# Turning residual rows without the pre-norm factor and applying that factor behind the matmuls

## The reference

```python
def rmsnorm(x, gain):
    return x * lax.rsqrt(jnp.mean(x * x, axis=-1, keepdims=True) + EPS) * gain

def first_block(x, ...):                       # MoBA attention + conv, then SwiGLU
    h = rms_norm(x, norm1_g);  proj = h @ w_in  # q, k, v, u
    x = x + jnp.concatenate([attn, conv], axis=-1) @ w_out
    h = rms_norm(x, norm2_g)
    return x + (jax.nn.silu(h @ w_gate) * (h @ w_up)) @ w_down

def second_block(x, ...):                      # i = 0: forgetting attention, i = 1: S5
    for i in range(2):
        h = rmsnorm(x, mix_pre_gain[i])
        m = fox_mixer(h, ...) if i == 0 else s5_mixer(h, ...)
        x = x + rmsnorm(m, mix_post_gain[i])
        h = rmsnorm(x, ffn_pre_gain[i])
        x = x + rmsnorm(swiglu(h, ...), ffn_post_gain[i])
    return x
```

## Time and profile before

| | us |
|---|---|
| median of 3 runs | 1075.32 (1074.3 to 1075.39) |
| profiled execution, its time | 1074.46 |
| its span | 1072.7 |
| mean granted clock, as a share of full speed | 0.978 |

### The profile page before, as it was taken

How to read it: one execution, slowest core, us unless ns; L and a number is a source line. 1 busy time by engine, 2 the same in 40 slices (tenths; PEclk the granted TensorE clock), 3 DMA queues, 4 the chain that set the end, 5 groups by cost and what they waited for, 6 DMA issues and landing times.

```text
span 1072.7 us, 16834 instructions
## 1 busy us (share of the span) xinstructions
PE 1018.6 (95%) x6908; PEld 894.5 (83%) x6908; DVE 610.5 (57%) x599; ACT 473.1 (44%) x606; POOL 356.3 (33%) x332
## 2 busy tenths in 40 slices
PE   7998799999999998989999999999968999999997
PEld 5985679999988786878779999987946979999986
DVE  3899665555564454553656854545566654554444
ACT  4762345444443455455454434334423554434432
POOL 4790057888889503120059900001030010000000
PEclk9999799999999999999999999999988999999999
DMA  9641025666667845454346566556961436556550
GB/s 353 204 155 52 1 83 178 206 205 206 220 231 231 245 136 180 126 169 151 105 140 194 157 196 194 168 194 208 395 232 41 157 119 196 168 185 195 181 172 39
DMA packets 130034, 186.85 MB, mean 174 GB/s; under 512 B 4672, under 2 KB 103488, under 8 KB 129344
## 3 DMA queue, kind: packets, MB, share of 16 engines
q1 hardware_dynamic: 105696, 158.34, 45.3%
q10 hardware_dynamic: 24288, 27.81, 7.8%
HBM read 174.60 MB, written 15.73 MB: 177 GB/s over the span
## 4 chain that ended last, share of the span: by engine, by line
PE 75%; DVE 12%; POOL 4%; issue 4%; ACT 3%; DMA 1%; POOLq 0%; SPq 0%; ACTq 0%; DVEq 0%
PE ps L363 11%; PE ps L365 11%; PE ps L364 11%; PE ps L406 7%; PE ps L410 7%; PE ps L408 7%; DVE cacc L1644 4%; PE ps L380 4%; PE ps L382 3%; PE ps L381 3%; DVE wlo L349 3%; PE ps L436 2%; POOL otmp L637 2%; ACT whi L343 2%; POOL ob L651 2%
## 5 line engine op out<-in xcount | busy, mean ns | idle before, releaser
L349 DVE TENSOR_TENSOR wlo<-wraw,whi 128x2048 fp32r<-128x2048 f32 x145 | 349.4, 2410 | 322.3 <-ACT whi L343 322.1
L343 ACT ACTIVATE whi<-wraw 128x2048 fp32r<-128x2048 f32 x145 | 277.5, 1914 | 282.0 <-PE ps L410 140.6
L363 PE MATMUL ps<-actH,whi 128*128 128x256 f32 x1248 | 356.3, 286 | 3.2 <-DVE actL L1921 2.1
L364 PE MATMUL ps<-actL,whi 128*128 128x256 f32 x1248 | 353.7, 283 | 0.0
L365 PE MATMUL ps<-actH,wlo 128*128 128x256 f32 x1248 | 353.6, 283 | 0.0
L363 PEld LDWEIGHTS ps<-actH,whi 128*128 128x128 f32 x1248 | 240.0, 192 | 6.8 <-issue 3.9
L364 PEld LDWEIGHTS ps<-actL,whi 128*128 128x128 f32 x1248 | 240.2, 192 | 0.0
L365 PEld LDWEIGHTS ps<-actH,wlo 128*128 128x128 f32 x1248 | 240.1, 192 | 0.0
L495 POOL TENSOR_SCALAR rs<-ss 128x1 f32<-128x1 f32 (+2 forms) x26 | 8.9, 341 | 605.8 <-ACT nat L478 485.3
L406 PE MATMUL ps<-whi,gH 128*128 128x512 f32 x264 | 82.0, 392 | 0.0
L408 PE MATMUL ps<-wlo,gH 128*128 128x512 f32 x264 | 81.3, 389 | 0.0
(11 more groups left out here) (312 smaller groups left out, 1372.2 us busy)
## 6 DMA issues: line engine op xcount, KB each, us to landing
wraw<-in_ffn_w_gate SPq DMA_DIRECT2D x22, 1024.0 KB, 5.3
wraw<-in_ffn_w_up SPq DMA_DIRECT2D x22, 1024.0 KB, 5.3
wraw<-in_ffn_w_down SPq DMA_DIRECT2D x22, 1024.0 KB, 5.0
wraw<-in_fox_w_in SPq DMA_DIRECT2D x16, 1024.0 KB, 5.4
wraw<-in_w_gate SPq DMA_DIRECT2D x11, 1024.0 KB, 5.3
wraw<-in_w_up SPq DMA_DIRECT2D x11, 1024.0 KB, 5.7
wraw<-in_w_down SPq DMA_DIRECT2D x11, 1024.0 KB, 5.1
wraw<-in_w_in SPq DMA_DIRECT2D x10, 1024.0 KB, 7.6
```

Source lines behind the costliest of these rows:

```text
L343: act.activation(self.whi[:, n0 % RING, :], self.wraw[:, n0 % RAW, :], ACT.Copy).then_inc(self.hi_done, 1)
L349: dve.tensor_tensor(self.wlo[:, n0 % RING, :], self.wraw[:, n0 % RAW, :], self.whi[:, n0 % RING, :].bitcast(F32), ALU.subtract).then_inc(s ...
L363: pe.matmul(out, wh, self.actH[:, k, :], start=(i == 0), stop=False)
L364: pe.matmul(out, wh, self.actL[:, k, :], start=False, stop=False)
```

## The change

`pe_turn_plain` transposes the residual rows as they are, so a turn starts when `x` is there, half a row block at a time (`x_ready` now counts halves). The last two tiles of r = 1 are turned inside the first unit's matmuls (`late`). The squares, the factor (kept in `rx`) and the diagonal come after the turn. In an FFN the factor of each token is spread over the partitions by one matmul with ones (`pe_spread`), between the two halves of the first up unit, copied out by ACT (`act_spread`), and multiplied into the gate bank before SiLU (`gscaled`); the down rows get the other factor in the squares' scale and in `dve_postnorm`. The forgetting attention takes `rx` as the scale of its evictions. S5's input is multiplied with the spread factor when it is written to `uT`, all by DVE. `keep_warm` at the turns gives way to short fills.

```diff
+    def pe_turn_plain(self, pe, st, ready, banks, warm=(4, 8)):
+        spare = self.tp_spot(KT - 1, banks)[:, (RT - 1) * P:RT * P]
+        def fill(count):
+            for _ in range(2 * count):
+                pe.matmul(spare, self.identb[:], self.identb[:], start=True, stop=True)
+        def one(kt, r):
+            last = pe.transpose(self.tp_spot(kt, banks)[:, r * P:(r + 1) * P],
+                                self.x[:, r, kt * P:(kt + 1) * P], self.ident[:])
+            if r == RT - 1:
+                last.then_inc(self.sem(st + "_transposed"), 1)
+        def late(kt):
+            pe.wait_ge(*self.past(st + "_act_ready", kt - 5))
+            one(kt, 1)
+        fill(warm[0])
+        for c, kts in ((1, (0, 1, 2, 3)), (2, (6, 7))):
+            pe.wait_ge(*self.past(ready, c))
+            for kt in kts:
+                one(kt, 0)
+        fill(warm[1])
+        pe.wait_ge(*self.past(ready, 3))
+        for kt in range(4):
+            one(kt, 1)
+        pe.wait_ge(*self.past(ready, 4))
+        for r in range(RT):
+            for kt in (4, 5):
+                one(kt, r)
+        return {2: lambda: late(6), 3: lambda: late(7)}
+
+    def pe_spread(self, pe, st, bank):
+        pe.wait_ge(*self.past(st + "_diag", RT))
+        pe.matmul(self.ps[:, bank, 0:TOK], self.ones[:], self.rdiag[:].rearrange("p r t -> p (r t)"),
+                  start=True, stop=True).then_inc(self.sem(st + "_spread"), 1)
+
+    def act_spread(self, act, st, bank):
+        act.wait_ge(*self.past(st + "_spread", 1))
+        act.activation(self.rdiag[:].rearrange("p r t -> p (r t)"), self.ps[:, bank, 0:TOK], ACT.Copy)\
+           .then_inc(self.sem(st + "_spread_out"), 1)
...
     def mm_features(...):
         for f in range(2):
             for i, k in enumerate(order):
+                if late and f == 0 and i in late:
+                    late[i]()
...
+            if f == 0 and middle:
+                middle()
     def pe_pair(...):
         if f0 > 0:
-            pe.wait_ge(*self.past(st + "_silu", f))
-        self.mm_features(pe, n0, a, it, ready)
+            pe.wait_ge(*self.past(st + "_gscaled", f))
+        self.mm_features(pe, n0, a, it, ready, late=late)
...
-        self.mm_features(pe, n0 + 1, a + 1, it)
+        self.mm_features(pe, n0 + 1, a + 1, it, middle=None if f0 > 0 else lambda: self.pe_spread(pe, st, 0))
     def act_pair(...):
-        act.wait_ge(self.used, n0 + 4 * it + 1)
-        if f0 > 0:
-            act.wait_ge(*self.past(st + "_prod", f))
-        act.activation(self.sg[:], self.ps[:, a, :], ACT.Silu).then_inc(self.sem(st + "_silu"), 1)
         self.split_high(act, n0 + 2, it)
+        act.wait_ge(*self.past(st + "_gscaled", f + 1))
+        act.activation(self.sg[:], self.sg[:], ACT.Silu).then_inc(self.sem(st + "_silu"), 1)
         self.split_high(act, n0 + 3, it)
     def dve_pair(...):
+        dve.wait_ge(self.used, n0 + 4 * it + 1)
+        if f0 > 0:
+            dve.wait_ge(*self.past(st + "_prod", f))
+        else:
+            dve.wait_ge(*self.past(st + "_spread_out", 1))
+        dve.tensor_tensor(sg, ps[a], rdiag spread over 2, ALU.mult).then_inc(self.sem(st + "_gscaled"), 1)
         self.split_low(dve, n0 + 2, it)
     def act_ffn(...):
+        self.act_spread(act, st, 0)
         self.over_pairs(...)
     def dve_postnorm(...):
-            dve.tensor_tensor(t, self.acc_row(base, r), g, ALU.mult).then_inc(self.sem(st + "_normed"), 1)
+            if st[:2] == "pf":
+                i = dve.scalar_tensor_tensor(t, self.acc_row(base, r), self.rx[:, r:r + 1], g, ALU.mult, ALU.mult)
...
-            dve.scalar_tensor_tensor(self.x[:, r, :], ...)
+            for c in range(2):
+                h = slice(512 * c, 512 * c + 512)
+                dve.scalar_tensor_tensor(self.x[:, r, h], ...).then_inc(self.sem(st + "_x_ready"), 1)
 tensor, f1 and fp (f2, s and f3 alike, with the default fills):
-            m.keep_warm(pe, 3, 8)
-            m.pe_turn(pe, "f1", (0, 1, 2, 3, 6, 7))
-            m.pe_ffn(pe, "f1", 4, prep=True)
-            m.keep_warm(pe, 4)
-            m.pe_turn(pe, "fp", (0, 1, 2, 3, 4, 5))
+            late = m.pe_turn_plain(pe, "f1", "f1_x_ready", (0, 1, 2, 3, 6, 7), (0, 5))
+            m.pe_ffn(pe, "f1", 4, late, prep=True)
+            pe.wait_ge(*m.past("prep_rout", NBLK))
+            pe.wait_ge(*m.past("prep_kout", NBLK))
+            late = m.pe_turn_plain(pe, "fp", "fp_x_ready", (4, 5, 6, 7, 2, 3), (0, 5))
 scalar, f1 and fp:
-            for r in range(RT):
-                m.act_squares(act, "f1", m.x[:, r, :], r, *m.past("f1_x_ready", r + 1))
+            m.split_high(act, 15)
             m.act_turn(act, "f1", (0, 1, 2, 3, 6, 7), gain=N2)
-            m.split_high(act, 15)
+            m.act_pre_squares(act, "f1", "f1_x_ready")
             m.act_ffn(act, "f1", 4, prep=True)
-            for r in range(RT):
-                m.act_squares(act, "fp", m.x[:, r, :], r, *m.past("fp_x_ready", r + 1))
+            m.split_high(act, first["fox"] + 1)
+            m.act_turn(act, "fp", (4, 5, 6, 7, 2, 3), gain=MIXPRE)
+            m.act_pre_squares(act, "fp", "fp_x_ready")
             (here come the DMAs of wf, fb and two gains)
-            m.act_turn(act, "fp", (0, 1, 2, 3, 4, 5), gain=MIXPRE)
             act.wait_ge(*m.past("wf_in", 16))
             act.activation(m.wfH[:], m.wf[:], ACT.Copy).then_inc(sem("wf_high"), 1)
 vector, S5 input:
+            dve.wait_ge(*m.past("s_spread_out", 1))
             for i in range(4):
-                if i % 2 == 1:
-                    dve.tensor_copy(m.uT[:, :, :, i, :], ...)     # ACT copied the even ones
+                dve.wait_ge(m.used, n + i + 1)
+                dve.tensor_tensor(m.uT[:, :, :, i, :], ps[:, i, :] ..., by_step ..., ALU.mult)
```

More of the change, by code:

```diff
@@ L350, in split_low, with mm_features @@
                           self.whi[:, n0 % RING, :].bitcast(F32), ALU.subtract).then_inc(self.lo_done, 1)
-    def mm_features(self, pe, n0, bank, it=0, ready=None, order=range(KT)):
+    def mm_features(self, pe, n0, bank, it=0, ready=None, order=range(KT), middle=None, late=None):
         pe.wait_ge(self.lo_done, n0 + 4 * it + 1)
@@ L384, in mm_quarter, with mm_half_k @@
             last.then_inc(self.used, 1)
-    def mm_half_k(self, pe, n0, banks, half, ready=None):
+    def mm_half_k(self, pe, n0, banks, half, ready=None, late=None):
         for k in range(4):
+            if late and k in late:
+                late[k]()
             self.mm_quarter(pe, n0, banks, half, k, ready)
@@ L479, in act_squares, with act_post_squares, act_pre_squares @@
            .then_inc(self.sem(st + "_squares"), 1)
-    def act_norms(self, act, post, pre, base, first, used):
+    def act_post_squares(self, act, st, base, first, used):
         for r in range(RT):
-            ready = self.past(first, 1) if r == 0 else (self.used, used)
-            self.act_squares(act, post, self.acc_row(base, r), r, *ready)
-        if pre:
-            for r in range(RT):
-                self.act_squares(act, pre, self.x[:, r, :], r, *self.past(post + "_x_ready", r + 1))
+            act.wait_ge(*(self.past(first, 1) if r == 0 else (self.used, used)))
+            act.activation(self.nat[:, r, :].rearrange("p (a b) -> p a b", a=2), self.acc_row(base, r), ACT.Square,
+                           scale=self.rx[:, r:r + 1] if st[:2] == "pf" else 1.0,
+                           accum_out=self.ss[:, r:r + 1]).then_inc(self.sem(st + "_squares"), 1)
+    def act_pre_squares(self, act, st, ready):
+        for r in range(RT):
+            self.act_squares(act, st, self.x[:, r, :], r, *self.past(ready, 2 * r + 2))
     def pool_rstd(self, pool, st, mean_of, ready, cols=None, out=None):
@@ L578, in over_pairs, with pe_ffn @@
                     prep(1 + j, it, 2)
-    def pe_ffn(self, pe, st, a, prep=False):
+    def pe_ffn(self, pe, st, a, late, prep=False):
         n = self.first[st + ".up"]
@@ L1271, in _ @@
                             (("fo_act_ready", 2 * i + 1),), first="o2_first" if i == 3 else None)
-            m.keep_warm(pe, 3)
-            m.pe_turn(pe, "f2", (0, 1, 2, 3, 6, 7))
-            m.pe_ffn(pe, "f2", 4)
-            m.keep_warm(pe, 7)
-            m.pe_turn(pe, "s", (4, 5, 6, 7, 2, 3))
-            for i in range(4):
-                m.mm_features(pe, first["s"] + i, i, ready="s_act_ready" if i == 0 else None)
-            pe.wait_ge(*m.past("ut_a", 2))
-            pe.wait_ge(*m.past("ut_d", 2))
+            late = m.pe_turn_plain(pe, "f2", "pm0_x_ready", (0, 1, 2, 3, 6, 7))
+            m.pe_ffn(pe, "f2", 4, late)
+            late = m.pe_turn_plain(pe, "s", "pf0_x_ready", (4, 5, 6, 7, 2, 3))
+            for i in range(4):
+                m.mm_features(pe, first["s"] + i, i, ready="s_act_ready" if i == 0 else None,
+                              late=late if i == 0 else None)
+                if i == 1:
+                    m.pe_spread(pe, "s", 4)
+            pe.wait_ge(*m.past("ut", 4))
             for h in range(2):
```

(21 more changed lines are left out.)

118 lines of the change are left out of this document (66 added, 52 removed), and 4 rows, old and new, of the table KINDS.

## The result

The changed kernel took 1078.7 us (median of 6 runs, 1078.46 to 1081.09) where the kernel before took 1075.12 in the same comparison (median of 6 runs). The ratio is 1.0038, with a 95% interval of 1.0023 to 1.0054: slower by 0.4%. The prediction was 1073.0 with a range of 1067.5 to 1077.5.

The account below looks back on a forecast made before the run. PE, busy 95% of the span, was taken as the bound, with the borders to win. Gains f2 1.5, s 3.1, f3 1.3 less f1 2.0, fp 1.4, clock risk 0.4, tail 0.2 gave 1.9 us: 1073.0, range 1067.5 to 1077.5.

Parts of the forecast that it names:

- the sum: Whole kernel: the stage terms, clock risk and tail added up to a gain of 1.9 us, 1073.0 us as forecast.
- D: Rival: POOL becomes the bound at the first FFN's odd preps, 1.5 us on each of five; 1080 us, chance 0.13.
- E: Rival: the clock falls at every turn, each of five borders losing up to 1.7 us; 1079 us, chance 0.08.
- The turn: Stage borders: first feature matmul 4.0 us earlier in the second and third FFN and s, 3.4 earlier at f1.
- f2: Second FFN: 1.5 us faster, bounds 0.5 slower to 2.4 faster, before a clock risk of 0.4 shared with the third.
- s: S5 stage: 3.1 us faster, from a turn 4.0 earlier and no stall, since the split is needed a unit later.
- f1: First FFN: 2.0 us slower, 0.9 from PE waiting 3.5 to 3.9 for POOL's prep 0 and 1.1 from the clock.
- fp: Forgetting attention: 4 us won are lost to a 4.1 us idle before the forget columns; clock makes it 1.4 slower.
- The first pair: Each FFN's first pair, second and third: PE waits 1.95 us because the split is queued behind the spread, which costs 0.47.
- The tail: End of the kernel: the halves of `x` and the scaled product add 0.2 us.
- B: Rival: f1 and fp come out well, prep 0 in time and one clock drop fails; 1068.8 us, chance 0.19.
- C: Rival: no stall at all, 4 us at each of five borders less 0.27 and 0.47 each; 1058 us, chance 0.03.

Follow-up runs that it names:

- e1: Changed kernel with `rx` laid over `rsk`, so every tile behind lies where it lay before the change; 1074.2 us against 1076.04, ratio 0.9977.
- e6: e1's kernel with ACT's and DVE's splits of unit n+2 ahead of the spread in each FFN's first pair; 1069.09 us against 1075.73, ratio 0.9938.
- e7: e1's kernel with the forget columns' DMA right behind f1 and their parts made before the turn's last two tiles; 1072.46 us against 1075.73, ratio 0.9965.
- e8: e1's kernel with POOL's memsets and prep 0 ahead of the factor of f1; 1069.07 us against 1075.73, ratio 0.9933.
- e9: e1's kernel with the edits of e6, e7 and e8 together; 1061.01 us against 1075.67, ratio 0.9864.
- e5: Not the kernel: groups of 24 matmuls alone, tiles at chosen places; 227 ns a matmul where both lie alike modulo 256 bytes, 229 to 234 otherwise.
- e11: As e5, 256 and 512 columns over more moving places for three stationary ones; 512 columns took 227 ns only where both lie alike.
- e12: e9's kernel with tiles reordered, no padding: `actH` and `actL` at 64 modulo 256 bytes, others at 128 as before; 1050.43 us against 1074.39, ratio 0.9773.
- e10: e9's kernel with an unused 64-byte tile ahead of `whi`, moving it and all behind it; 1053.23 us against 1075.67, ratio 0.977.
- e2: The kernel before with 64 unused bytes behind `rsk` and nothing else changed; ratio 1.0032.
- e3: The kernel before with 128 unused bytes behind `rsk`; ratio 1.0033.

## Why the prediction was wrong

**The failed step is the sum.** It held every term of time and no term of place. `rx` was read as a factor kept in a tile, and not as 64 bytes ahead of gH, gL and yoH. That term is worth 5.6 us in the stages (37 units of 5.44 us became some 5.60) and about 5.4 in the runs (e1). Without it the change measures -1.8 us (e1: 1074.2 against 1076.04, with -4.0 to -0.9 as the interval), where the sum said -1.9. That they stand so near is in part luck, since the terms below missed by up to 1.5 us each and offset each other. No rival held the place: D and E, the two slower ones, are not what happened, and that E's 1079 is next to the measured 1078.7 is chance.

**The turn, forecast 4.0 us earlier:** 3.83, 3.82 and 3.95 at f2, s and f3, 3.36 at f1 (forecast 3.4), 4.20 at fp (forecast 4.25). Right.

**The first pair, forecast a wait of 1.95 us:** matmuls start 2.0 us apart at 568.1 and 890.8, of which 1.74 us count as idle. e6 shows that the order of split and spread is the whole of it: with the splits ahead the wait is gone and f3's pairs took 127.41 us, 0.6 more than before the change, of which the prediction has 0.47 for the spread. f3 came out at -1.33, forecast -1.3.

**f2, forecast -1.5:** measured 0. The mechanism was right, and the clock was mis-sized: it fell behind this idle, 1.7 us, of which I had counted 0.4 for f2 and f3 together. "Near the stretch that was left alone" was the weak reason. The same idle let the clock fall in f2 of the changed kernel, e1 and e7 and not in f2 of e8 (130.21 us), and in f3 of e1 (130.90 us, 0.62 in a window of 4 us), e7 and e8 and not in f3 of the changed kernel. A forecast can only give it a chance.

**s, forecast -3.1:** -2.9 until `uT` is used. The time from there to the S5 gate units grew by 0.6. It lies in the 128 small matmuls that read `Uall` (3.6 us until the transposes of `Vc`, then 4.2); no wait that the trace names stands behind it, and it is there in e6 too, where the tiles lie as before. Its cause stays open.

**f1, forecast +2.0:** +1.5 for border and pairs together. PE waited 3.54 us (forecast 3.5 to 3.9), POOL's first step took 1.61 us and prep 0's last 3.33, each beside a split. The Trainium skill ("SBUF — State Buffer", "SBUF: two separate sides") would have them exclude each other for a whole instruction; these rows agree with it, and so do e6's of 3.23 and 3.50 us. e8, which moves prep 0 out of the way, made the pairs 4.2 us shorter than in the changed kernel: the wait and the clock's fall behind it, less a wait of 0.9 for a split that now shows. The 178.9 for the second gate unit before is 178.67 in the trace.

**fp, forecast +1.4:** +0.9, with two errors that offset. The idle was 2.1 us and not 4.1, since the DMA went out ahead of the first square and not behind it, and the half unit ended a little later. The clock fell as forecast, but the time from the forget columns to the end of o2 grew by 2.6 us, where 1.4 was forecast. In e7, with neither the idle nor the fall, it is still 0.9 longer than before; the cause of that stays open.

**The tail, forecast +0.2:** +0.29. Of the span's 4.24 us more, 5.59 are the down and o3 units. All the rest is -1.35, of which -0.35 lies in the first block, which the change does not touch; so the terms of the sum come to about -1.0 in this pair of executions.

**The rivals.** B and C, the two faster ones, did not come about: the waits were all there. D, which is about the later, odd preps, is refuted. Of the waits in f1 from 162 to 375 us (total, times, longest) one is prep 0's 3.5 us, so the others sum to 1.4, against 2.1 in the earlier trace rows:

```profile
PE ps L734 <- POOL ob L724: 4.9, 5, 3.5
```

E is refuted too: the clock was 1.00 in the turns. By the Trainium skill ("TensorE: Matmul & The Clock Gate", "Part 4: PE-mode transpose") a turn made of transposes should not hold the clock; at 873.6 to 878.6 it did, though short bf16 matmuls filled part of that stretch, so the rule itself was not isolated here.

## What to carry to other kernels

A new tile is not free where others lie behind it: read the places of the matmuls' operands before and after, as one reads the waits, and put a new small tile into dead space, as e1 did, or last (not tried here). Where a stage that a diff doesn't touch changes its length by a steady few per cent and nothing waits, compare the number of matmuls in equal windows before looking at engines or transfers. And a factor moved behind a product must not stand, in an engine's order, ahead of a split that the next unit needs: that move of order was worth 4.8 us (e6 against e1), and with the forget columns early and prep 0 ahead of the factor 12.8 (e9 against e1).

## What the runs showed that I had not expected

- The pace of a stream of fp32 matmuls depends on where stationary and moving operand lie to each other modulo 256 bytes: for 512 columns 227 ns alike, 229 to 234 otherwise; for 256 columns 120 alike or with moving 96 above, and 113.3 to 119 for the others (e5, e11). It needs no other engine at work.
- For 256 columns this is worth more than the whole change did without its misplaced tile (9.3 us, e12 against e9, and 1.8): the ratio to the kernel before went from 0.9864 (e9) to 0.9773 (e12), with no instruction more or fewer.
- The same places can run at two steady paces, 113.3 and 117.8 ns. A short idle of PE stood at two of the switches (e12 at 608.8, e10 at 607) and none at a third (e10 at 601.5). What chooses between them stays open; it was not tried further. A 117.8 in the map, as for (64, 0), may then be the slower pace of a place that has a quicker one.
- An idle of PE of 1.74 us let the clock fall in some places and executions and not in others, so single stages differ by 1.5 us from run to run. So did the idle of 2.58 us in the attention of fp (a fall in the kernel before, none in e2 and e3).
